# Odd weight tiles of the expert layers split on GpSimd instead of VectorE

## The reference, cut to what matters

```python
def peer(xn, wq, k1, k2, u_tab, v_tab):
    q = (xt @ wq).reshape(t, PEER_HEADS, D_KEY)          # 8 heads, keys of 2 x 128
    s1, s2 = ...                                         # scores against 128 + 128 half keys
    v1, i1 = lax.top_k(s1, TOPK); v2, i2 = lax.top_k(s2, TOPK)      # TOPK = 16
    sv, ci = lax.top_k(v1[..., :, None] + v2[..., None, :], TOPK)
    experts = e1 * N_KEYS + e2                           # of 16384 experts
    gates = jax.nn.softmax(sv, axis=-1)
    hid = jax.nn.gelu(jnp.einsum("td,tkd->tk", xi, u_tab[ei]))
    return jnp.einsum("tk,tkd->td", gi * hid, v_tab[ei])
```

## Time and profile before

| | |
|---|---|
| median of 3 runs | 4177.67 us (4173.7 to 4180.77) |
| the profiled execution | 4183.87 us, span 4182.1 us |
| PE matmul busy | 3718.4 us (89%) |
| DVE busy | 2493.1 us (60%), of it 846.9 us in 692 weight splits |
| ACT busy | 1389.9 us (33%), of it 822.0 us in 788 casts |
| POOL busy | 330.4 us (8%), of it 247.2 us in 96 weight splits |
| granted TensorE clock, mean | 0.934 of full speed |

### The profile page before, as it was taken

How to read it: one execution, slowest core, us unless ns; L and a number is a source line. 1 busy time by engine, 2 the same in 40 slices (tenths; PEclk the granted TensorE clock), 3 DMA queues, 4 the chain that set the end, 5 groups by cost and what they waited for, 6 DMA issues and landing times.

```text
span 4182.1 us, 69766 instructions
## 1 busy us (share of the span) xinstructions
PE 3718.4 (89%) x26672; PEld 3370.6 (81%) x26672; DVE 2493.1 (60%) x4018; ACT 1389.9 (33%) x2128; POOL 330.4 (8%) x216
## 2 busy tenths in 40 slices
PE   7779789999999887989999999997876999799898
PEld 6479789999999765978998999985644787587698
DVE  5349765766786552886566577845474323464544
ACT  3234224233223333332332422243242223332443
POOL 1237100000000011640000000000000000000000
PEclk9789999999999987999999999998988999899999
DMA  6434324334333544442432433341101222221153
GB/s 233 164 101 153 104 96 166 101 127 140 102 111 130 174 166 148 133 144 95 138 128 100 166 101 105 110 155 49 47 1 41 80 97 96 71 86 53 54 177 131
DMA packets 131673, 478.33 MB, mean 114 GB/s; under 512 B 14512, under 2 KB 16560, under 8 KB 130992
## 3 DMA queue, kind: packets, MB, share of 16 engines
q1 hardware_dynamic: 115696, 416.72, 29.7%
q0 software_dynamic: 15808, 59.25, 4.2%
HBM read 474.87 MB, written 1.05 MB: 114 GB/s over the span
## 4 chain that ended last, share of the span: by engine, by line
PE 75%; DVE 16%; issue 3%; ACT 2%; DMA 2%; POOL 0%; DVEq 0%; ACTq 0%; SPq 0%
PE bank L426 74%; DMA HA<-mods 1%; ACT Wh L853 1%; DVE arena L1400 1%; DVE arena L1555 1%; DVE arena L1397 1%; DVE arena L1421 1%; DVE Wl L1218 1%; DVE arena L1396 1%; DVE arena L1399 1%; DVE arena L1398 1%; PE bank L667 1%; DVE arena L1477 1%; DVE arena L1442 1%; DVE arena L1439 1%
## 5 line engine op out<-in xcount | busy, mean ns | idle before, releaser
L426 PE MATMUL bank<-HR,Wh 128*128 128x256 f32 (+1 forms) x12288 | 1849.2, 304 | 157.8 <-DVE HR L1550 60.0
L426 PEld LDWEIGHTS bank<-HR,Wh 128*128 128x128 f32 x12288 | 1661.2, 196 | 244.4 <-issue 74.7
L1218 DVE TENSOR_TENSOR Wl<-ring,Wh 128x1024 fp32r<-128x1024 f32 x692 | 846.9, 1225 | 1221.7 <-ACT Wh L853 1221.0
L853 ACT CAST Wh<-ring 128x1024 fp32r<-128x1024 f32 x788 | 822.0, 1043 | 856.7 <-PE bank L426 853.6
L426 PE MATMUL bank<-HR,Wl 128*128 128x256 f32 (+1 forms) x6144 | 952.9, 298 | 13.8 <-DVE Wl L1218 7.5
L426 PEld LDWEIGHTS bank<-HR,Wl 128*128 128x128 f32 x6144 | 848.9, 194 | 44.7 <-DVE Wl L1218 7.9
L426 PE MATMUL bank<-arena 128*128 128x32 f32 (+5 forms) x4576 | 643.6, 296 | 95.5 <-issue 46.9
L426 PEld LDWEIGHTS bank<-arena 128*128 128x128 f32 (+3 forms) x4576 | 553.3, 194 | 165.9 <-issue 101.4
L1014 ACT ACTIVATE arena<-bank 128x256 f32 x256 | 98.1, 383 | 805.7 <-PE bank L426 805.5
L1477 DVE TENSOR_TENSOR arena<-arena,K 128x1024 f32<-128x1024 f32 x256 | 311.3, 1216 | 0.1
L1701 POOL TENSOR_TENSOR Wl<-ring,Wh 128x1024 fp32r<-128x1024 f32 x96 | 247.2, 2587 | 145.6 <-ACT Wh L853 145.4
(11 more groups left out here) (214 smaller groups left out, 1966.3 us busy)
## 6 DMA issues: line engine op xcount, KB each, us to landing
ring<-weights SPq DMA_DIRECT2D x788, 512.0 KB, 3.3
HA<-mods POOLq DMA_DIRECT2D x96, 512.0 KB, 6.2
arena<-bias POOLq DMA_DIRECT2D x16, 256.0 KB, 2.9
arena<-keys POOLq DMA_DIRECT2D x2, 1024.0 KB, 5.5
HA<-mla POOLq DMA_DIRECT2D x1, 1536.0 KB, 6.5
K<-constants SPq DMA_DIRECT2D x1, 1402.0 KB, 6.1
X<-x SPq DMA_DIRECT2D x1, 1024.0 KB, 8.6
X<-context POOLq DMA_DIRECT2D x1, 1024.0 KB, 7.2
```

Of the source, the lines that this page charges most:

```text
L426: return nc.tensor.matmul(out, lhsT, rhs, start=first, stop=last)
L853: nc.scalar.copy(Wh[:, i % SPL], ring[:, i % RAW]).then_inc(S("hi_done"), 1)
L1218: v.tensor_tensor(Wl[:, i % SPL], ring[:, i % RAW], Wh[:, i % SPL], ALU.subtract).then_inc(S("lo_done"), 1)
```

## The change

Every odd tile of the expert stretches behind u0 is split on POOL, the even ones stay on DVE. The same holds for the one odd tile among the first three behind each expert block, whose casts are issued in the last steps of it. Tiles of wq and u0 stay on POOL. In place of `lo_done` there are two counters, `lo_dve` and `lo_pool`; `LOW[i]` says which engine has tile i and `LOW_COUNT[i]` how many parts that engine has finished with it. PE and SP wait on the counter of the tile's own engine, and neither splitting engine waits for the other any more. SP's one loop becomes a loop for each stretch whose pattern repeats.

```diff
-POOL_TILES = [(l * N1 + N_IN + N_OUT, l * N1 + N_IN + N_OUT + N_WQ + EQ) for l in range(L)]
+P0 = N_IN + N_OUT + N_WQ
+def low_engine(i):
+    l, j = divmod(i, N1)
+    if l < L and N_IN + N_OUT <= j < P0 + EQ:
+        return "pool"
+    if (l < L and j >= P0 + EQ or 1 <= l <= L and j < LEAD) and i % 2:
+        return "pool"
+    return "dve"
+LOW = [low_engine(i) for i in range(NTILES)]
+LOW_COUNT = [LOW[:i + 1].count(LOW[i]) for i in range(NTILES)]
...
+        def wait_low(eng, i, it=0):
+            step = LOW_COUNT[min(i + R, NTILES - 1)] - LOW_COUNT[i]
+            eng.wait_ge(S(f"lo_{LOW[i]}"), LOW_COUNT[i] + step * it)
...
-            for i in range(R):
-                after(sp, S("lo_done"), i - RAW + 1)
-                load(i, i % RAW)
-            with sp.Fori(1, total // R) as it:
-                for s in range(R):
-                    sp.wait_ge(S("lo_done"), it * R + (s - RAW + 1))
-                    load(it * R + s, s % RAW)
...
+            for i in range(RAW):
+                load(i, i)
+            def stream(a, b):
+                n = (b - a) // R if LOW[a:b] == LOW[a:a + R] * ((b - a) // R) + LOW[a:a + (b - a) % R] else 0
+                if n:
+                    with sp.Fori(0, n) as it:
+                        for s in range(R):
+                            wait_low(sp, a + s, it)
+                            load(it * R + (a + s + RAW), s % RAW)
+                for i in range(a + n * R, b):
+                    wait_low(sp, i)
+                    load(i + RAW, i % RAW)
+            for l in range(L):
+                a = l * N1
+                stream(a, a + N_IN + N_OUT)
+                stream(a + N_IN + N_OUT, a + P0 + EQ)
+                stream(a + P0 + EQ, a + N1)
+            stream(MOD0, MOD0 + RAW)
+            stream(MOD0 + RAW, NTILES - RAW)
...
-                pe.wait_ge(S("lo_done"), i + 1 + R * it)
+                wait_low(pe, i, it)
...
-                    if any(a <= i < b for a, b in POOL_TILES):
+                    if LOW[i] == "pool":
                         lo_next[0] += 1
                         continue
-                    if any(i == b for _, b in POOL_TILES):
-                        dve.wait_ge(S("lo_done"), i)
                     dve.wait_ge(S("hi_done"), i + 1 + R * it)
-                    v.tensor_tensor(Wl[:, i % SPL], ring[:, i % RAW], Wh[:, i % SPL], ALU.subtract).then_inc(S("lo_done"), 1)
+                    v.tensor_tensor(Wl[:, i % SPL], ring[:, i % RAW], Wh[:, i % SPL], ALU.subtract).then_inc(S("lo_dve"), 1)
...
-                a, b = POOL_TILES[n]
-                pool.wait_ge(S("lo_done"), a)
...
+            def rest(i, it=0):
+                pool.wait_ge(S("hi_done"), i + 1 + R * it)
+                nc.gpsimd.tensor_tensor(Wl[:, i % SPL], ring[:, i % RAW], Wh[:, i % SPL], ALU.subtract)\
+                    .then_inc(S("lo_pool"), 1)
+            def rests(l):
+                for a, b in ((N_IN + N_OUT, P0 + EQ), (P0 + EQ, N1)):
+                    def body(it, a=l * N1 + a):
+                        for s in range(R):
+                            if LOW[a + s] == "pool":
+                                rest(a + s, it)
+                    steps(pool, (b - a) // R, False, body)
+                for i in range((l + 1) * N1, (l + 1) * N1 + LEAD):
+                    if LOW[i] == "pool":
+                        rest(i)
```

More of the change, by code:

```diff
@@ L405, in load @@
                              wts[bass.ds(i, 1), :, :].rearrange("o p n -> (o p) n")).then_inc(S(f"tile{slot}"), 16)
-            total = NTILES if stop_after is None else stop_after
-            for i in range(R):
-                after(sp, S("lo_done"), i - RAW + 1)
-                load(i, i % RAW)
-            with sp.Fori(1, total // R) as it:
-                for s in range(R):
-                    sp.wait_ge(S("lo_done"), it * R + (s - RAW + 1))
-                    load(it * R + s, s % RAW)
-            for i in range(total // R * R, total):
-                sp.wait_ge(S("lo_done"), i - RAW + 1)
-                load(i, i % RAW)
+            for i in range(RAW):
[17 more added lines that the diff above has]
+            stream(MOD0 + RAW, NTILES - RAW)
             sp.wait_ge(S("res_ev"), OUT_RES)
@@ L458, in token_tile @@
                 w = high(i)
-                pe.wait_ge(S("lo_done"), i + 1)
+                wait_low(pe, i)
                 for tt in range(tts):
@@ L1691, in _ @@
         def _(pool):
-            def rests(n):
-                a, b = POOL_TILES[n]
-                pool.wait_ge(S("lo_done"), a)
[L1697 to L1703, removed]
+            def rest(i, it=0):
[12 more added lines that the diff above has]
+                        rest(i)
             pool.wait_ge(S("const_in"), 16)
```

## The result

| | before | after |
|---|---|---|
| median | 4177.28 us (4 runs, 4173.7 to 4180.77) | 4265.06 us (4 runs, 4260.85 to 4268.26) |
| the profiled execution | 4183.87 us | 4267.54 us |

The ratio is 1.021, 95% interval 1.0194 to 1.0227: 2.1% slower. 4260 us had been forecast.

What follows compares the result with a forecast made beforehand. Chains of waits between PE, ScalarE's cast and DVE were taken to bound the expert loops; 103.5 - 18.9 - 2.3 = +82.3 us on 4183.9 gave 4266.2, as a median 4260 us, range 4225 to 4330.

Steps and rivals of the forecast that it cites:

- v0, v1, v3: Ungated expert stretches: line 1499 waits out POOL's subtraction before each odd tile, 1.15 us on 90 pairs, +103.5 us.
- u2, u3 and v2: Gated stretches: the even chain keeps 10.25 us a pair in u2, u3; v2's PE time covers the delay; 0.
- u1's table load: First step of each u1 body: ScalarE's 1.28 us table load no longer delays DVE, whose split goes to POOL; -18.9 us.
- u0: End of u0: one of DVE's three splits in a row ahead of the softmax sums goes to POOL; -2.3 us.
- Queues: SP's later wait on POOL's counter covered by 4.9 us; the context load behind tile 601 lands before its first reader.
- The signs named: Profile after: v0, v1, v3 about 116 us, PE idles 1.2 to 1.3, line 1499's median far over 0.42.
- No block at the port: Rival: DVE and POOL don't exclude each other, line 1499 is early before odd tiles; -21.2, 4157 us; chance 0.09.
- Faster gated loops: Rival: u1 to u3 come down to PE's own time, up to 0.83 us on 96 pairs, -80, 4180 us; chance 0.07.
- A falling clock: Rival: PE's recurring idles in ungated stretches lower the granted clock, +54 to +108, 4314 to 4368 us; chance 0.11.

Runs made afterwards that it cites:

- dve_later: Kernel before, every split on DVE, but in u1 to v3 DVE splits tile s + 2 in step s instead of tile s + 3: 4045.0 us, ratio 0.9675.
- u_all_pool: All splits of u1 to u3 on POOL, v0 to v3 on DVE, orders as in the kernel before: 4072.13 us, ratio 0.9753 to the kernel before.
- psum_operand: Whole change, but in v0, v1, v3 line 1499 reads a PSUM bank instead of the SBUF high part: 4151.15 us, ratio 0.9932 to kernel before.

## Why the prediction was right

- *v0, v1, v3* (103.5 forecast, 101.4 measured). Step by step: 1.12 + 2.40 + 0.28 + 0.05 = 3.85 us, measured 3.85; the pair 7.02, measured 7.02. The wait of line 1499 is shown by the exchange of one operand, and its end 0.28 us behind POOL's held for all 126 blocked instances.
- *u2, u3 and v2* (0). Measured +2.5 us over both layers: u2 and u3 +3.6, v2 -1.1. The middle bodies of u2 and u3 are at 41.5 to 41.9 as before, but for those with a slow piece of PE (below), which take up to 43.3; v2 is at PE's own pace. PE's idle is gathered before every second tile, as foreseen. Line 1508 is blocked up to 2.63 us there, as foreseen too, and no body shows a cost. That half the splits bring none of the period is shown from both sides, by `dve_later` and `u_all_pool`. What the prediction left out is that POOL waits as well, in u2 for instance:

```profile
765.26 1.21 DVE L1505 TENSOR_TENSOR arena<-arena,K 128x1024 f32<-128x1024 f32 x1
765.75 2.98 POOL L1723 TENSOR_TENSOR Wl<-ring,Wh 128x1024 fp32r<-128x1024 f32 x1 [7.27 <-ACT Wh L883]
766.39 2.61 DVE L1508 TENSOR_TENSOR arena<-arena,K 128x256 f32<-128x256 f32 x1
```

  POOL's split is issued while the one-hot of line 1505, with two SBUF inputs, is running, and takes 2.98 us instead of its 2.40; then line 1508 (0.42 us alone) is the one that waits. In u1 to u3 after, POOL's splits have medians of 2.98 to 3.07 us, in v0, v1 and v3 2.39. So the one that is issued second waits, whichever it is. For POOL this is read from the rows; no run takes an input of line 1505 away.
- *u1's table load* (-18.9, measured -14.0). The mechanism was right, the size was not. Bodies came down from 44.3 to 41.8, but one in each layer still took 43.1. It has a slow piece of PE (granted clock 0.85 over it), in the chain in order of time after, with an idle of only 0.77 us ahead of it:

```profile
534.24 11.06 PE bank L456 x80
```

  I had tied these pieces to the long idles alone, and had them all vanish.
- *u0* (-2.3, measured -1.6). Two splits in a row instead of three, in the place where PE waits for DVE.
- *Queues.* ScalarE's casts waited 3.2 us for weights over the whole run, before and after. The context load was issued at 2887.53 and its first reader starts at 2911.07; no wait for it shows.
- *The signs named.* v0 and v1 at 116.8 to 117.3 us came, and a blocked line 1527. Three came otherwise. PE's idle before every second tile is 1.01 us, not 1.2 to 1.3. The median of line 1527 stayed at 0.43 us, as a little under half of its instances wait. DVE's busy time was to fall by much less than 278 us and rose by 132.6: its waits for POOL, which count as busy, are worth some 411 us (an estimate, 278 + 132.6), most of them off PE's path.
- *The sum.* The terms add up to +88.3 by the casts against +82.3 forecast: +2.5, +4.9 and +0.7 too low, 2.1 too high. The medians say +87.8. Most of the miss is the slow pieces: the chain before has eight (six in u1, two in u2 and u3), the one after six, where the sum had two left. Four more at 1.2 us (11.04 against 2 x 4.92) are 4.9 us, an estimate. That the term of v0, v1 and v3 erred the other way, so that 6 us are missing and not 8, is luck.
- *The rivals.* No block at the port: out by the 2.30 us instances and by `psum_operand`. Faster gated loops: out for half the splits, yet what I gave 0.83 us a pair is 1.1 once the chain is broken (10.40 to 9.29). A falling clock: out, v0 ran at 1.00 with an idle of 1.01 us in each 7.02.

## What to carry to other kernels

Before work is moved to an idle engine, find out whether the loaded engine's work or its order holds the loop: if each step starts a few hundredths of a microsecond after the same instruction, while the engine of that instruction is idle for a part of each step (DVE was busy 52 of 99 us in v0), suspect the order. The test is to change the order and leave the work as it is: let the engine first take up a tile whose input is already there. Here that was worth 3.2%, and 226 splits on another engine nothing beside it. An instruction moved to GpSimd that reads SBUF, as these splits do, should be laid where no two-input VectorE instruction at the end of a chain falls into its 2.4 us; if it can't be, give that instruction an input from PSUM or make its input earlier. Both of these worked here.

## What the runs showed that I had not expected

- Eight small gate matmuls and 24 tile matmuls take 4.65 us a tile on PE when nothing holds it (37.17 / 8), in u1 to u3 as in v2; the kernel before took 5.2 in u2 and u3.
- PE idles of 1.01 us in each 7.02 left the granted clock at 1.00 from v0's second pair to its end, while a slow piece of 11.04 to 11.07 us turns up once in each gated u stretch, where most idles are 0.6 to 0.9 us a pair. What starts them stays open.
- The stretch ahead of the first expert block, where all kernels here do the same work on the same engines, took between 320 and 333 us from the first cast to the 48th. That alone is up to 0.3% between two single profiles, so the change is better read from its own stretches.
